# A hybrid gMLP and differential-attention layer: attention steps in pairs with VectorE tasks placed by an account of its time, and the first loads led by x block 0

## What is computed

```python
mod = silu(c) @ w_ada + b_ada;  shift, scale, gate = split(mod, 3)
h = rms_norm(x, norm_w) * (1 + scale) + shift
u_a, v_a, z_a, q, k, v, z_b = split(h @ w_in, 7)            # 512 columns each
# group A: chunks of 128 positions, 4 heads
a = u_a * (tril(w_s) @ rms_norm(v_a) + b_s) * silu(z_a)
# group B: 4 heads, two query/key components of 64, values of 128, causal
q, k = rope(rms_norm(q)), rope(rms_norm(k))
o = (softmax(q1 k1^T / 8) - lam * softmax(q2 k2^T / 8)) @ v
b = rms_norm(o, subln_w) * (1 - lam_init) * silu(z_b)
out = x + gate * (concat(a, b) @ w_out)
```

## Time and profile before

| | us |
|---|---|
| median of 3 runs | 525.61 (525.59 to 526.62) |
| profiled execution | 526.04 |
| its slowest core, span | 524.6 (core 4; the others 514.8 to 523.1) |
| busy in the span: PE, DVE, ACT, POOL | 445.6, 334.7, 299.2, 88.6 |
| busy share of PE, DVE, ACT, POOL | 85%, 64%, 57%, 17% |
| HBM read, written | 50.29 MB, 8.39 MB |

### The profile page before, as it was taken

The page is one execution under the profiler, slowest core; times in us unless marked ns, Lnnn a source line. Parts: engine busy times, 40 slices in busy tenths (PEclk is TensorE's granted clock), DMA queues, the critical chain, the costliest instruction groups (busy, mean ns, idle before and its releaser), DMA issues.

```text
span 524.6 us, 9798 instructions; the slowest of 8 cores (514.8 to 524.6 us)
## 1 busy us (share of the span) xinstructions
PE 445.6 (85%) x3104; PEld 217.6 (41%) x3104; DVE 334.7 (64%) x761; ACT 299.2 (57%) x402; POOL 88.6 (17%) x118
## 2 busy tenths in 40 slices
PE   0037679899999999999998999979997999999396
PEld 0002224344443444444445555445554555555242
DVE  1246732682775468888873767788558757868732
ACT  1066456545554227777767666666778778677100
POOL 1113440000671000000001112222222222122100
PEclk9997869899999999999999999979998999999879
DMA  8999978007624300021021122194140131011013
GB/s 200 251 308 257 311 240 180 0 1 131 167 87 139 121 1 2 1 47 36 1 81 41 42 81 60 62 282 202 47 156 2 39 100 67 22 62 42 40 63 139
DMA packets 15606, 53.90 MB, mean 103 GB/s; under 512 B 2242, under 2 KB 2626, under 8 KB 14660
## 3 DMA queue, kind: packets, MB, share of 16 engines
q1 hardware_dynamic: 13924, 45.36, 26.0%
q0 software_dynamic: 1152, 7.50, 8.3%
q10 hardware_dynamic: 480, 0.41, 0.3%
HBM read 50.29 MB, written 8.39 MB: 112 GB/s over the span
## 4 chain that ended last, share of the span: by engine, by line
PE 60%; DVE 11%; DMA 9%; issue 7%; ACT 6%; POOL 5%; DVEq 0%; SPq 0%; ACTq 0%; POOLq 0%
PE psum L647 15%; PE psum L470 13%; PE psum L1049 8%; PE psum L927 7%; DMA sb_WO<-w_adaT 5%; PE psum L897 5%; ACT sb_cs L910 3%; DMA sb_kT<-xT 3%; PE psum L1015 3%; POOL sb_cs L915 3%; DVE sb_F L984 3%; DVE sb_F L943 1%; PE psum L677 1%; PE psum L675 1%; PE psum L667 1%
## 5 line engine op out<-in xcount | busy, mean ns | idle before, releaser
L910 ACT ACTIVATE sb_cs<-psum,sb_small 128x1024 bf16<-128x1024 f32 x144 | 150.9, 1113 | 58.6 <-PE psum L897 55.2
L927 PE MATMUL psum<-sb_vB,sb_cs 128*128 128x129 bf16 x1088 | 89.5, 226 | 9.7 <-DVE sb_F L943 5.2
L927 PEld LDWEIGHTS psum<-sb_vB,sb_cs 128*128 128x128 bf16 x1088 | 64.4, 100 | 40.5 <-issue 40.1
L470 PE MATMUL psum<-sb_W,sb_hT 128*128 128x512 bf16 x256 | 65.8, 420 | 17.5 <-ACT sb_hT L466 15.4
L915 POOL TENSOR_TENSOR sb_cs<-sb_cs,sb_constb 128x256 bf16<-128x256 bf16 x64 | 44.5, 697 | 213.3 <-ACT sb_cs L910 208.7
L647 PE MATMUL psum<-sb_hT,sb_W 128*128 128x512 bf16 x280 | 65.8, 379 | 0.0
L897 PE MATMUL psum<-sb_qT,sb_kT 64*128 64x256 bf16 (+1 forms) x576 | 56.4, 274 | 6.9 <-ACT sb_cs L910 4.7
L470 PEld LDWEIGHTS psum<-sb_W,sb_hT 128*128 128x128 bf16 x256 | 26.4, 105 | 56.2 <-issue 34.1
L357 DVE SCALAR_TENSOR_TENSOR sb_F<-sb_WO,sb_F 128x1024 f32<-128x1024 f32 x24 | 30.2, 1257 | 30.5 <-DMA sb_WO<-w_adaT 22.0
L647 PEld LDWEIGHTS psum<-sb_hT,sb_W 128*128 128x128 bf16 x280 | 27.3, 98 | 30.0
L436 PE MATMUL psum<-sb_vnA,sb_constb 128*128 128x512 bf16 x32 | 11.9, 507 | 30.5 <-ACT sb_vnA L429 30.5
(11 more groups left out here) (114 smaller groups left out, 548.4 us busy)
## 6 DMA issues: line engine op xcount, KB each, us to landing
sb_WO<-w_adaT SPq DMA_DIRECT2D x24, 512.0 KB, 8.1
sb_W<-w_in POOLq DMA_DIRECT2D x5, 1024.0 KB, 9.9
sb_W<-x SPq DMA_DIRECT2D x8, 512.0 KB, 4.4
sb_cs<-w_out SPq DMA_DIRECT2D x8, 512.0 KB, 3.4
sb_hT<-x SPq DMA_DIRECT2D x8, 512.0 KB, 12.0
out<-sb_hT SPq DMA_DIRECT2D x8, 512.0 KB, 2.6
out<-sb_W SPq DMA_DIRECT2D x6, 512.0 KB, 2.8
sb_qT<-xT SPq DMA_DIRECT2D x4, 512.0 KB, 23.4
```

The source lines that it names most:

```text
L470: pe(lambda E: E.matmul(PS(bank), lhsT=hT[:, kc, 128 * tt:128 * (tt + 1)], rhs=wsl[slot][:, kc, :], start=(kc == 0), stop=(kc == KC - 1)), ...
L910: act(lambda E: E.activation(out=et, in_=psum[:, X:X + 2, :], func=AF.Exp, bias=negM, scale=0.125), reads=[pb[X], pb[Y], b_lam], writes=[b ...
L927: pe(lambda E, u=u, j=j, c=c, i=i: E.matmul(psum[:, j, 256 * c:256 * c + 129], lhsT=et[:, c, QB * u + 128 * j:QB * u + 128 * (j + 1)], rhs ...
```

## The change

Head: x block 0 is loaded first, then c and the w_adaT tiles; the first w_in slice waits for x block 0; the ones of the sum of squares are written on chip; `mod_kc` is two VectorE operations; Silu of c comes after `phaseA(0)`; the z_B slice waits for the 14th w_adaT tile. `prepB` gives every second `phaseB` to ScalarE and is cut into quarters.

Attention: the loop takes two steps at once (two exponentials, two query-key steps, then fillers, then two probability-value steps). Fillers are issued by single matmuls, 4.8 a pair on average. `group_end` copies only component 0 and reads the rest from PSUM; `uu`, `rc`, `sso`, `rso` have four buffers in place of three. VectorE tasks have a cost, and `tasks` issues one while the account `tdv` plus its cost stays before the next group's end, w_out tasks when no other is left. After the loop fillers have six banks, and five tiles are issued ahead of the last transposes.

```diff
@@ -370,15 +370,18 @@
     for qt in range(4):
         P.dma("act", posc[32 * qt:32 * (qt + 1), :], pos1[512 * qt:512 * (qt + 1)].partition_broadcast(32),
               b_pos[qt], writes=[b_pos[qt]])
+    load_xT(0)
     P.dma("sp", c_bc, c_d.rearrange("a n -> (a n)").partition_broadcast(128), b_F[0], writes=b_c)
-    P.dma("pool", constb[:, :], cb_d, b_constb, writes=[b_constb])
     ADA = []
     for kc in range(KC):
         ADA += [kc, 8 + kc]
-    for j in ADA[0:4]:
-        load_ada(j, (0, 1, 2, 3))
-    load_xT(0)
-    load_w(0, G_VB)
+    ada_dma = [load_ada(j, (0, 1, 2, 3)) for j in ADA[0:4]]
+    load_w(0, G_VB, extra=[x_last[0]])
+    P.dma("pool", constb[:, :], cb_d, b_constb, writes=[b_constb])
+    load_xT(1)
+    ones_t = sb("ones_t", [128, 128], BF16)
+    b_ones = buf("ones_t")
+    dve(lambda E: E.memset(ones_t[:, :], 1.0), writes=[b_ones])
 
     dve(lambda E: E.memset(epsn, NORM_EPS), writes=[b_sc])
     dve(lambda E: E.memset(epss, SUBLN_EPS), writes=[b_sc])
...
          reads=[b_small], writes=[b_bada1])
...
         if n + 4 < 16:
-            load_ada(ADA[n + 4], (0, 1, 2, 3))
+            ada_dma.append(load_ada(ADA[n + 4], (0, 1, 2, 3)))
 
     def mod_kc(kc):
-        pool(lambda E: E.tensor_tensor(out=shift[:, kc:kc + 1], in0=modraw[:, kc:kc + 1], in1=bada[:, kc:kc + 1], op=ALU.add),
-             reads=[b_small, b_raw_[kc]], writes=[b_mod[kc]])
-        pool(lambda E: E.tensor_tensor(out=gvec[:, kc:kc + 1], in0=modraw[:, 8 + kc:9 + kc], in1=bada1[:, kc:kc + 1], op=ALU.add),
-             reads=[b_bada1, b_raw_[8 + kc]], writes=[b_mod[kc]])
-        pool(lambda E: E.tensor_tensor(out=gvec[:, kc:kc + 1], in0=gvec[:, kc:kc + 1], in1=normw[:, kc:kc + 1], op=ALU.mult),
-             reads=[b_small, b_mod[kc]], writes=[b_mod[kc]])
+        dve(lambda E: E.tensor_tensor(out=shift[:, kc:kc + 1], in0=modraw[:, kc:kc + 1], in1=bada[:, kc:kc + 1], op=ALU.add),
+            reads=[b_small, b_raw_[kc]], writes=[b_mod[kc]])
+        dve(lambda E: E.scalar_tensor_tensor(out=gvec[:, kc:kc + 1], in0=modraw[:, 8 + kc:9 + kc], scalar=bada1[:, kc:kc + 1],
+                                             in1=normw[:, kc:kc + 1], op0=ALU.add, op1=ALU.mult),
+            reads=[b_bada1, b_small, b_raw_[8 + kc]], writes=[b_mod[kc]])
+
+    def pair(kc):
+        mv(2 * kc)
+        mv(2 * kc + 1)
+        mod_kc(kc)
 
     def start_mm(tb, kc):
         phaseB(tb, kc, "act")
@@ -500,37 +506,36 @@
             vb_main(tt, tt % 8, kc)
 
     phaseA(0)
-    mv(0)
-    mv(1)
-    load_xT(1, (0, 1))
-    mv(2)
-    mv(3)
-    load_xT(1, (2, 3))
-    mv(4)
-    mv(5)
+    act(lambda E: E.activation(out=c_bc, in_=c_bc, func=AF.Silu), reads=b_c, writes=b_c)
+    phaseM(0, 0)
+    phaseM(0, 1)
+    pair(0)
+    start_mm(0, 0)
+    phaseM(0, 2)
+    phaseM(0, 3)
+    pair(1)
+    start_mm(0, 1)
+    phaseA(1)
+    pair(2)
+    start_mm(0, 2)
+    pair(3)
+    start_mm(0, 3)
+    phaseM(1, 0)
+    phaseM(1, 1)
+    pair(4)
+    start_mm(0, 4)
     for kc in range(3):
-        mod_kc(kc)
-    for q in range(4):
-        phaseM(0, q)
-    for kc in range(2):
+        start_mm(1, kc)
+    phaseM(1, 2)
+    phaseM(1, 3)
+    for kc in range(5, 8):
+        pair(kc)
         start_mm(0, kc)
-    phaseA(1)
-    start_mm(0, 2)
-    for i in range(5):
-        kc = 3 + i
-        mv(2 * kc)
-        mv(2 * kc + 1)
-        mod_kc(kc)
-        if i < 4:
-            phaseM(1, i)
-        start_mm(0, kc)
-        for k1 in ((0, 1), (2, 3), (4, 5), (6,), (7,))[i]:
+        for k1 in ((3, 4), (5, 6), (7,))[kc - 5]:
             start_mm(1, k1)
-        if i == 0:
-            load_w(1, G_ZB)
-        if i == 4:
-            for tt in range(4):
-                vb_evac(tt, tt)
+    for tt in range(4):
+        vb_evac(tt, tt)
+    load_w(1, G_ZB, extra=[ada_dma[13]])
     load_xT(2)
     load_xT(3)
     for s_ in (0, 1):
@@ -728,11 +733,10 @@
         dve(lambda E: E.tensor_scalar(out=nlam, in0=nlam, scalar1=-LAM_INIT, scalar2=None, op0=ALU.add),
             reads=[b_lam], writes=[b_lam])
 
-    def prepB(tb):
-        for q in range(4):
-            phaseM(tb, q)
-            phaseB(tb, 2 * q, "dve")
-            phaseB(tb, 2 * q + 1, "dve")
+    def prepB(tb, q):
+        phaseM(tb, q)
+        phaseB(tb, 2 * q, "dve")
+        phaseB(tb, 2 * q + 1, "act")
 
     def zb(tt):
         step(make_tile(G_ZB, tt, 1))
@@ -745,13 +749,11 @@
     for q in range(4):
         phaseMM(2, q)
     phaseLn(2)
-    prepB(2)
-    zb(5)
-    phaseSq(3, 0)
-    zb(6)
-    phaseSq(3, 1)
-    zb(7)
-    phaseSq(3, 2)
+    prepB(2, 0)
+    for q in range(3):
+        zb(5 + q)
+        prepB(2, q + 1)
+        phaseSq(3, q)
     drain()
     phaseSq(3, 3)
     for kc in range(KC):
@@ -761,9 +763,12 @@
             for q in range(4):
                 phaseMM(3, q)
             phaseLn(3)
-    prepB(3)
+    prepB(3, 0)
+    prepB(3, 1)
     for tt in range(8, 12):
         vb_evac(tt, tt % 4)
+    prepB(3, 2)
+    prepB(3, 3)
     for kc in range(KC):
         for tt in range(12, 16):
             vb_main(tt, 4 + tt % 4, kc)
...
 
-    raw = [carve(520).rearrange("p (j c x) -> p j c x", j=2, c=2) for _ in range(2)]
-    uu = [carve(1024).rearrange("p (j h d) -> p j h d", j=2, h=4) for _ in range(3)]
-    sqo = [carve(128) for _ in range(2)]
+    raw = [carve(264).rearrange("p (j x) -> p j x", j=2)] * 2
+    uu = [carve(1024).rearrange("p (j h d) -> p j h d", j=2, h=4) for _ in range(4)]
+    sqo = [carve(128)] * 2
     fin = [carve(512).bitcast(BF16).rearrange("p (j n) -> p j n", j=2) for _ in range(2)]
-    b_rw = [bufs("raw%d_" % a, 2) for a in range(2)]
...
+            assert uu_owner.get(b) is None, (jq, h)
+            uu_owner[b] = jq
         O4 = psum[:, 0:2, :].rearrange("p j (c x) -> p j c x", c=2)
-        for j in range(2):
-            dve(lambda E, j=j: E.tensor_copy(out=raw[a][:, j, :, 0:129], in_=O4[:, j, :, 0:129]),
-                reads=[pb[j]], writes=[b_rw[a][j]])
-        dve(lambda E: E.reciprocal(out=rc[b][:, h], in_=raw[a][:, :, :, 128]), reads=b_rw[a], writes=[b_rc[b][h]])
-        dve(lambda E: E.scalar_tensor_tensor(out=snl[a], in0=rc[b][:, h, :, 1], scalar=nlam, in1=raw[a][:, :, 0, 128],
+        dve(lambda E: E.tensor_copy(out=raw[a][:, :, 0:129], in_=O4[:, :, 0, 0:129]), reads=pb[0:2], writes=b_rw[a])
+        dve(lambda E: E.reciprocal(out=rc[b][:, h], in_=O4[:, :, :, 128]), reads=pb[0:2], writes=[b_rc[b][h]])
+        dve(lambda E: E.scalar_tensor_tensor(out=snl[a], in0=rc[b][:, h, :, 1], scalar=nlam, in1=raw[a][:, :, 128],
                                              op0=ALU.mult, op1=ALU.mult),
             reads=b_rw[a] + [b_rc[b][h], b_lam], writes=[b_snl[a]])
         for j in range(2):
             dve(lambda E, j=j: E.scalar_tensor_tensor(
-                out=uu[b][:, j, h, :], in0=raw[a][:, j, 1, 0:128], scalar=snl[a][:, j:j + 1], in1=raw[a][:, j, 0, 0:128],
-                op0=ALU.mult, op1=ALU.add), reads=[b_rw[a][j], b_snl[a]], writes=[b_uu[b][h]])
+                out=uu[b][:, j, h, :], in0=O4[:, j, 1, 0:128], scalar=snl[a][:, j:j + 1], in1=raw[a][:, j, 0:128],
+                op0=ALU.mult, op1=ALU.add), reads=[pb[j], b_snl[a]] + b_rw[a], writes=[b_uu[b][h]])
+
         def squares():
...
-        taskq.append(squares)
+                later(now[0] + 3, lambda: block_norm(jq))
+                later(now[0] + 5, lambda: taskq.append((0.3, lambda: norm_scale(jq))))
...
         act(lambda E: E.activation(out=rso[b], in_=rso[b], func=AF.Exp, scale=-0.5), reads=[b_rso[b]], writes=[b_rso[b]])
+
+    def norm_scale(jq):
+        b = bpar[jq]
         dve(lambda E: E.tensor_tensor(out=rso[b], in0=rso[b], in1=rc[b][:, :, :, 0].rearrange("p h j -> p j h"), op=ALU.mult),
             reads=[b_rso[b]] + b_rc[b], writes=[b_rso[b]])
-        for h in range(4):
-            taskq.append(lambda h=h: run_fin(jq, h))
+        for h_ in range(4):
+            taskq.append((0.85, lambda h_=h_: run_fin(jq, h_)))
+
+    uu_owner = {}
 
     def run_fin(jq, h):
         fin_head(jq, h)
         if h == 3:
+            uu_owner[bpar[jq]] = None
             later(now[0] + (2 if now[0] < NS else 0), lambda: fill_front(("tr", lambda bank: transposes(jq, bank, range(4)), 0.6)))
 
     def fin_head(jq, h):
...
+    def fill(n):
+        while n > 0 and (cur or fillq):
+            if not cur:
+                open_tile()
+            kind, mms, bank, post = cur[0]
+            if kind == "tr":
+                n += 1
+            while mms and n > 0:
+                mms.pop(0)()
+                n -= 1
+            if not mms:
+                cur.pop()
+                posts.append((bank, post))
...
+    tpe, tdv = [0.0], [0.0]
+
+    def dv(cost):
+        tdv[0] = max(tdv[0], tpe[0]) + cost
+
+    def next_end(gs):
+        t, g = tpe[0], gs
+        while g < NS:
+            t += 1.2
+            if gsteps[g][4]:
+                return t
+            g += 1
+        return 1e9
+
+    def tasks(limit, force=99):
```

(97 more changed lines are left out.)

94 lines of the change are left out of this document (50 added, 44 removed).

## The result

The changed kernel takes **559.4 us** (median of 4 runs, 556.3 to 561.1), the kernel before 525.6 us: ratio 1.063, 95% interval 1.057 to 1.070. It is slower by 6.3% where 501 us was forecast.

What follows compares the result with a forecast made beforehand. The prediction saw DMA bounding the head, no engine full in attention, and the norm chain holding the tail. 526.04 - 6 (head) - 8.6 (loop) - 10.2 (tail) = 501.2 us, said as 501; range 483 to 516.

Steps and rivals of the forecast that it cites:

- DMA is the resource: Head: DMA transfers set the pace; the last block-0 scaling comes at 58.5 us, 12 us earlier than 70.54.
- 16.2 MB at 300 GB/s: Head: bytes needed before the last w_adaT tile, at the rate read from the old profile: 54 us, 55 with the start.
- rival D: Head: z_B slice lands at 70 us and ScalarE's added scalings eat the rest; head gain 0, 507 us; chance 0.1.
- ScalarE's share of the scalings: Head: four scalings of 0.81 us moved to ScalarE and a wait of about 1.2 us add 4.4 us.
- 72 pairs of 2.58 us: Attention loop: PE's work per pair (query-key, probability-value and 4.8 filler matmuls) sets the pace, 185.8 us in all.
- w_out stall 6 us: Attention loop: first three w_out tasks each wait for their load on in-order VectorE; PE stands 6 us for the bank.
- Group ends at 0.2 us, 6 us: Attention loop: PE waits 0.2 us at each of 32 group ends, where banks are held 1.85 us; 6 us.
- So a punctual VectorE costs nearly nothing: Attention loop, group ends: query-key and filler work (0.58 + 1.04 us) or 6.8 fillers (1.5 us) cover PE during the bank hold.
- Pairs "nearly the same" as steps: Attention loop: the forecast's "nearly the same" compared PE's 2.58 us a pair with ScalarE's about 2.5 us.
- The combination from PSUM at most 0.06 us dearer: Attention loop, group ends: reading PSUM costs 0 to 0.06 us more per combine, 0.03 taken; 13 us of copies saved.
- C: Rival, attention loop: PE stands 1.3 us at each of 32 group ends, loop 242 us, kernel 537 us; chance 0.05.
- The clock: Whole kernel: prediction called wrong if PE's granted clock falls in stretches where it now stays up; no size given.

Runs made afterwards that it cites:

- e10: Kernel before with the changed head, z_B slice issued behind the tenth w_adaT tile instead of the 14th: 526.7 us, ratio 1.010 to the kernel before.
- e12: Kernel before with the changed head, all scalings of x blocks 2 and 3 on VectorE, none on ScalarE: 524.7 us, ratio 1.006 to the kernel before.
- e4: Changed kernel with the eight w_out scalings at fixed pairs 5 to 21: 553.8 us on cores 4 to 7, ratio 1.067 to the kernel before.
- e15: e9 with the eight w_out scalings at fixed pairs 5 to 21: 547.2 us, ratio 1.046 to the kernel before, loop 226.1 us.
- e13: Kernel before, step order kept, with the changed group end, whose combination reads PSUM: 524.4 us, ratio 1.004, loop 213.2 us.
- e6: Changed kernel with row sums and both components copied from PSUM to SBUF before the combination: 560.2 us, ratio 1.074 to the kernel before.
- e7: Changed kernel with norm later for six blocks and sums copied out of PSUM first; leaves out the last block's end: loop 225.7 us.
- e9: Changed kernel with the norm four steps later for six blocks and an ending that issues everything: 548.3 us, ratio 1.050 to the kernel before.
- e14: e9 with value products one step behind the exponentials, plus related filler and task placing: 552.8 us, ratio 1.060 to the kernel before.
- e17: e15 with filler matmuls handed out by need (8, 6 or 2.6 a pair) instead of 4.8: 549.6 us, ratio 1.052 to the kernel before.
- e8: Kernel before with the changed ending alone (norm chain first, five tiles ahead of the last transposes, six banks): 512.5 us, ratio 0.9825.

## Why the prediction was wrong, step by step

**Head, forecast 6 us won; measured 7.8 lost in the changed kernel (9 alone).** Three terms failed. (1) "DMA is the resource", and with it "16.2 MB at 300 GB/s". Over the first 63 us core 4 moved 250 GB/s (264 before) and core 1 238 (257); these rates count a w_in slice at its landed size, by which the forecast's 300 is the kernel before's 271 of the first 75 us. The last block-0 scaling came at 64.7 us on core 1 and 67.4 on core 4, not 58.5. The bytes ahead of the last tile were fewer, but they could not be asked for in time. The fifth w_adaT tile took 17 us to land, as x block 1 and the slice shared the way; then twelve dot products stood in VectorE's queue with the products of x block 1, VectorE was full from 40 to 57 us, and the DMA engines, with only four slots to fill, were 0.76 busy on core 4 where they had been 0.96. The forecast gave VectorE 3.5 us behind the last tile ("one or two queued ones") and no place as the limit. (2) The z_B slice, put at 51 us issued and 65 landed, was issued at 57.25 and used from 73.3: rival D's place, 70 us, was nearer. e10 prices its lateness at 4 us. (3) ScalarE's share of the scalings, put at 4.4 us, cost 6 (e12: 110.16 against 104.06). The mechanism was right and undersized by 1.7 us. V_B's tiles 8 to 11 were evacuated from 107.4 us on core 4, not 98.

**Loop, forecast 8.6 us won; measured 33.5 lost.** My own stretch, first score product to last value product, is 277.72 to 531.2 us on core 4: 253.5 us, forecast 206.6. By its terms:

- *72 pairs of 2.58 us.* Right as a floor (2.52 and 2.62 above), wrong as a mean. A sum of engine times is a lower bound; I took it for the time.
- *w_out stall 6 us.* The stall was 4.96 us, where forecast. It is worth 2.0 (e4) to 3.5 us (e15).
- *Group ends at 0.2 us, 6 us.* PE waited 21.1 us at 23 places, 0.66 us an end. The held bank as such is worth 3.3 us (e13; 3.2 and 4.1 by e6 and e7), so the duration of the hold was priced well. What failed is "So a punctual VectorE costs nearly nothing" and the 0.2 us an end: twelve short groups put two ends one to three steps apart, and between the value products of one pair lies at most the filler.
- *The norm.* It had no term at all. I added up VectorE's load, and did not follow who waits for it on another engine: two ScalarE instructions, which the pair loop issues right behind the next pair's exponentials, with all later exponentials behind them. 13.8 us by e9 (some 11 without the moved work), the largest single item.
- *Pairs "nearly the same" as steps.* With norm and w_out mended they are 12.9 us longer (e15 against e13). e14 and e17 show that lag and filler, as I changed them, don't remove it. That it is the order as such is one reading and no run isolated it; the account that places VectorE's tasks, and filler in single matmuls, differ between e15 and e13 too. Which of these it is stays **open**. (13.8, 3.5, 12.9 and 3.3 make up the 33.5 because the runs form one chain: each is a difference of two loops in it.)
- *The combination from PSUM at most 0.06 us dearer.* The mean is 350 ns where it was 383 from SBUF: not dearer. The Trainium skill, VectorE: DVE Perf Modes, section Rules for kernel authors, advises the copy where many operations follow. It came out on the rule's side, though not for the operation's speed: the copy frees banks sooner, 3 to 4 us of loop here.

**The clock**, named among what would make the prediction wrong, did fall: 0.91 in the loop against 0.97, and filler matmuls of 512 columns took 0.41 us in the mean instead of 0.38. With two levels, 0.91 of 245.1 us means some 44 us at the lower one, and 0.97 of 210.8 us some 13. It followed the gaps, since e15, with the longest waits gone, has 0.96. It is a second price of the same waits: PE is busier by 4.5 us for the same matmuls, and by estimate the price is up to 11 us, half of the 35 us for which PE was busy at the lower level less half of the 13 before. It is a part of the items above, not a further one: as means of the eight cores, in e4 PE's idle time is unchanged (46.7 us against 46.6) and its busy time 2.2 us less, which is all that w_out gave there; in e9 the idle time is 6.8 us less and the busy time 7.0, of which 2.3 is moved work.

**Tail, forecast 24.1 us after the last value product; measured 24.1** (531.2 to 555.3 us, core 4), with PE busy ahead of the transposes and then waiting 2.6 us where 3 were forecast. e8 shows that it stands alone.

**The rivals.** C had the sign and nearly its loop (242 us; the measured loop of 243.4 is of another cut), with a chance of 0.05. Its mechanism, 1.3 us at each of 32 ends, was not it: half of that is measured, and the rest came from the norm, which no rival had, and from what stays open. D was right on the head and still too mild. My range, 483 to 516, left C out; that C alone had the sign was luck, as its wait was half of what it needed.

## What to carry to other kernels

When a change moves the order of tasks on one engine, list for each what waits on another engine and what is queued behind that waiter; a sum of busy times per pair is a floor and says nothing of this. A long wait at a buffer may be only where a lateness arrives: free the buffer early and see whether the time moves; here half of a 21 us wait went and the loop was 3 us shorter. A load that is held back must leave enough other loads to ask for: count the slots and who frees them. Work that fills the last chain of dependent steps, kept back for it, is a gain by itself, here 10 us, and can be taken without the rest.

## What the runs showed of the hardware

A load among others is not priced by its bytes alone: w_adaT tiles of 512 KB took 9.7 us in the median to land in the first 66 us of core 1 (12.1 on core 4; in the kernel before 11.5 and 11.2), against 5.7 over the whole run of core 1, and the fifth 17. VectorE's combination of 128 columns with one input in PSUM took 350 ns, with all in SBUF 383. And the granted clock depends on where idle time lies, not only on its sum: on cores 1 to 3 PE was idle 36.7 to 38.6 us of the loop in e14 and 35.9 to 38.2 in e15, and the clock was 0.92 to 0.93 in the one and 0.95 to 0.96 in the other. In the changed kernel it fell to 0.50 behind a wait of 1.79 us and in one of 4.96 us. The Trainium skill, TensorE: Matmul & The Clock Gate, section Part 1, says that an idle array falls back to 1.2 GHz and comes up again under load; the rows agree, with 0.50 from 293.80 to 300.60 us and 1.00 behind it.
